# Feed-forward products with the high and low input halves side by side, 512 columns at a time

## The reference

```python
def swiglu(x, w_in, w_out):
    gate, up = jnp.split(x @ w_in, 2, axis=-1)
    return (jax.nn.silu(gate) * up) @ w_out

h = swiglu(rmsnorm(x, norm_ffn1_pre[l]), w_ffn1_in[l], w_ffn1_out[l])
x = x + FFN_RESIDUAL_SCALE * rmsnorm(h, norm_ffn1_post[l])
```

## Time and profile before

| | |
|---|---|
| median of 3 runs | 1515.03 us (1514.87 to 1515.17) |
| the profiled execution's own time | 1514.94 us |
| its span, first to last instruction | 1513.3 us |
| granted TensorE clock, mean of the span | 1.000 |
| the nine pairs of the first stage | about 60 to 241 us of the span |
| the nine pairs of the second stage | about 635 to 816 us |

### The profile page before, as it was taken

The page is one execution under the profiler, slowest core; times in us unless marked ns, Lnnn a source line. Parts: engine busy times, 40 slices in busy tenths (PEclk is TensorE's granted clock), DMA queues, the critical chain, the costliest instruction groups (busy, mean ns, idle before and its releaser), DMA issues.

```text
span 1513.3 us, 23600 instructions
## 1 busy us (share of the span) xinstructions
PE 1497.9 (99%) x9156; PEld 1343.9 (89%) x9156; DVE 1071.1 (71%) x1279; ACT 744.2 (49%) x1102; POOL 54.2 (4%) x101
## 2 busy tenths in 40 slices
PE   8999999999999999999999999999999999999998
PEld 7899998889988889899999888788888888889997
DVE  5888885326856847888886665788888865736873
ACT  6545443226566427544444234567676633344554
POOL 1000000001200002000000000100000000000001
PEclk9999999999999999999999999999999999999999
DMA  6233323232232222233335663222223132322331
GB/s 198 84 112 101 96 81 140 89 105 84 69 103 84 82 101 69 87 109 93 102 111 195 236 208 84 57 65 74 57 82 83 56 111 84 112 85 87 107 112 56
DMA packets 135044, 153.33 MB, mean 101 GB/s; under 512 B 3728, under 2 KB 123660, under 8 KB 134972
## 3 DMA queue, kind: packets, MB, share of 16 engines
q1 hardware_dynamic: 131712, 137.38, 28.9%
q0 software_dynamic: 3024, 14.88, 2.9%
q10 hardware_dynamic: 236, 0.06, 0.0%
HBM read 150.08 MB, written 2.23 MB: 101 GB/s over the span
## 4 chain that ended last, share of the span: by engine, by line
PE 96%; DVE 2%; ACT 1%; issue 0%; DMA 0%; DVEq 0%; ACTq 0%
PE ps L2532 20%; PE ps L2697 20%; PE ps L2534 19%; PE ps L2533 19%; PE ps L2702 10%; PE ps L2897 1%; PE ps L3003 1%; PE ps L3013 1%; PE ps L2983 1%; PE ps L2982 1%; PE ps L3012 1%; PE ps L2615 0%; PE ps L2964 0%; PE ps L2675 0%; DVE wl L1544 0%
## 5 line engine op out<-in xcount | busy, mean ns | idle before, releaser
L2532 PE MATMUL ps<-ah,wh 128*128 128x512 f32 (+1 forms) x1136 | 431.7, 380 | 3.8 <-DVE wl L1945 1.4
L2534 PE MATMUL ps<-ah,wl 128*128 128x512 f32 (+1 forms) x1136 | 425.6, 375 | 0.0
L2533 PE MATMUL ps<-al,wh 128*128 128x512 f32 (+1 forms) x1136 | 425.2, 374 | 0.0
L1544 DVE TENSOR_TENSOR wl<-raw,wh 128x2048 fp32r<-128x2048 f32 x59 | 135.2, 2291 | 191.2 <-ACT wh L831 191.0
L2532 PEld LDWEIGHTS ps<-ah,wh 128*128 128x128 f32 x1136 | 213.9, 188 | 43.3 <-issue 2.3
L2534 PEld LDWEIGHTS ps<-ah,wl 128*128 128x128 f32 x1136 | 213.8, 188 | 38.9
L2533 PEld LDWEIGHTS ps<-al,wh 128*128 128x128 f32 x1136 | 214.1, 188 | 35.5
L831 ACT ACTIVATE wh<-raw 128x2048 fp32r<-128x2048 f32 x60 | 114.7, 1911 | 236.7 <-PE ps L2534 233.0
L2697 PE MATMUL ps<-al,wh 128*128 128x256 f32 x704 | 172.7, 283 | 0.0
L2697 PE MATMUL ps<-ah,wh 128*128 128x256 f32 x704 | 172.7, 283 | 0.0
L2697 PEld LDWEIGHTS ps<-al,wh 128*128 128x128 f32 x704 | 135.2, 192 | 0.1
(11 more groups left out here) (436 smaller groups left out, 2535.6 us busy)
## 6 DMA issues: line engine op xcount, KB each, us to landing
raw<-in_w_ffn_in SPq DMA_DIRECT2D x74, 512.0 KB, 3.6
raw<-in_w_in SPq DMA_DIRECT2D x52, 512.0 KB, 4.4
raw<-in_w_ffn_out SPq DMA_DIRECT2D x22, 1024.0 KB, 5.0
ada_raw<-in_w_ada POOLq DMA_DIRECT2D x8, 1536.0 KB, 7.2
raw<-in_w_mix_in SPq DMA_DIRECT2D x10, 1024.0 KB, 5.4
raw<-in_w_ffn_in SPq DMA_DIRECT2D x7, 1024.0 KB, 5.3
raw<-in_w_in SPq DMA_DIRECT2D x6, 1024.0 KB, 5.6
raw<-in_w_mix_out SPq DMA_DIRECT2D x4, 1024.0 KB, 5.0
```

The source lines that it names most:

```text
L1544: nc.vector.tensor_tensor(wl[n % 2][:], raw[n % 2][:], wh[n % 2][:].bitcast(fp32), ALU.subtract).then_inc(lo_done, 2 if n + 1 in AHEAD else 1)
L2532: nc.tensor.matmul(bank, w[0], m[0], start=start, stop=False, skip_group_check=shared)
L2533: nc.tensor.matmul(bank, w[0], m[1], start=False, stop=False, skip_group_check=shared)
L2534: return nc.tensor.matmul(bank, w[1], m[0], start=False, stop=stop, skip_group_check=shared)
```

## The change

For the two feed-forward stages (not for the pairs of the second block), the high and the low input stand side by side in one buffer. In B11, T2, T3 and T4 one matmul of 512 columns takes both, high to the left and low to the right half of a whole bank; the low weight's matmuls go to the left half. So the result stands in two banks (0 and 1, or 6 and 7, one for each 128 result columns) and in two sides, which have to be added:

- for up1 and gate1 ScalarE copies both sides out, and GpSimd adds the second to the first (`sides`);
- for gate2 VectorE joins in two steps, the second waiting for the first (`sided_join`);
- for the last product ScalarE copies the low side to a new tile `whole2` (`last_side`), VectorE adds the high side, waits for that, and multiplies.

B22, T1 and B21 stay as they are. The out slot's first pass takes the banks in another order. The core of the diff:

```diff
+SIDE = 6
-        ah = sb("ah", [P, KD, T], f32r)
-        al = sb("al", [P, KD, T], f32r)
+        both = sb("both", [P, 2, KD, T], f32r)
+        ah, al = both[:, 0], both[:, 1]
...
+            both_sums = sb("both_sums", [P, 2, 3, KD // 2, T // 2], f32r, where=phase)
+            sh, sl = both_sums[:, 0], both_sums[:, 1]
+            whole2 = sb("whole2", [P, 2, T // 2], where=phase)
+        up1_side, gate1_side = (tile[:].rearrange("p (c t) -> p c t", c=2) for tile in (acc, h7))
...
+        def high_side(par):
+            return ps[:, SIDE * par:SIDE * par + 2, 0:T // 2]
+        def low_side(par):
+            return ps[:, SIDE * par:SIDE * par + 2, T // 2:T]
+        def both_of(f, name):
+            if name == "T3":
+                return both_sums[:, :, 1, :, :]
+            low, high = slice(0, KD // 2), slice(KD // 2, KD)
+            return both[:, :, high if name == "T4" else low, COLS[name != "B11"]]
@@ GpSimd @@
+            def sides(f):
+                first = SEVEN_AT[f]
+                def added(i, n, step, tile, side):
+                    pool.wait_ge(copied, i * 6 + (3 * n + step))
+                    nc.gpsimd.tensor_tensor(tile[:], tile[:], side, ALU.add).then_inc(side_added, 1)
+                def pair(i, par):
+                    n = first + par
+                    added(i, n, 1, up1, up1_side)
+                    added(i, n, 3, gate1, gate1_side)
...
+            sides(0)
             pool.wait_ge(rlo_done, 2)
...
             add_residual(3)
+            sides(1)
@@ ScalarE @@
+                def last_side(i, par):
+                    act.wait_ge(hid_ready, i * 2 + (f * NFO + PLAIN[f] + par))
+                    nc.scalar.activation(whole2[:], low_side(par % 2), ACT.Copy).then_inc(side_copied, 1)
+                    def sided_product(target, side):
+                        nc.scalar.activation(target[:], high_side(par % 2), ACT.Copy)
+                        nc.scalar.activation(side, low_side(par % 2), ACT.Copy).then_inc(copied, 1)
                         used(0)
+                        last_side(i, par - 1)
-                    product(up1, BANK1[par % 2])
+                    sided_product(up1, up1_side)
-                    product(gate1, BANK1[par % 2])
+                    sided_product(gate1, gate1_side)
...
                 act.wait_ge(p_used, PRODS * (last + 1))
+                last_side((SEVEN[f] - 1) // 2, (SEVEN[f] - 1) % 2)
                 hi(base_out + 1)
@@ VectorE, hidden(), second half @@
-                        nc.vector.tensor_tensor(at, ps[:, BANK1[par % 2], :].rearrange("p (c t) -> p c t", c=2), at, ALU.mult).then_inc(hid_ready, 1)
+                        dve.wait_ge(side_copied, i * 2 + (n + 1))
+                        nc.vector.tensor_tensor(whole2[:], high_side(par % 2), whole2[:], ALU.add).then_inc(last_joined, 1)
+                        dve.wait_ge(last_joined, i * 2 + (n + 1))
+                        nc.vector.tensor_tensor(at, whole2[:], at, ALU.mult).then_inc(hid_ready, 1)
@@ VectorE, pair() @@
+                    def sided_join(tile):
+                        nc.vector.tensor_tensor(tile[:], high_side(par % 2), tile[:], ALU.add).then_inc(high_joined, 1)
+                        dve.wait_ge(high_joined, i * 2 + (n + 1))
+                        nc.vector.tensor_tensor(tile[:], low_side(par % 2), tile[:], ALU.add).then_inc(joined, 1)
                     dve.wait_ge(copied, i * 6 + (3 * n + 3))
+                    dve.wait_ge(side_added, i * 4 + (2 * n + 2))
                     join(gate1, BANK5)
-                    join(gate2, BANK1[par % 2])
+                    sided_join(gate2)
@@ TensorE @@
+            def sided(f, i, n, k, par):
+                moving = both_of(f, PRODUCTS[k])
+                for nb in range(2):
+                    for kk in range(KD // 2):
+                        nc.tensor.matmul(ps[:, SIDE * par + nb, :].rearrange("p (s t) -> p s t", s=2), ring_of(wh, f, k)[:, kk, nb * P:(nb + 1) * P],
+                                         moving[:, :, kk, :], start=k == 0 and kk == 0, stop=False, skip_group_check=True)
+                pe.wait_ge(p_lo, i * 2 * PRODS + (PRODS * n + k + 1))
+                for nb in range(2):
+                    for kk in range(KD // 2):
+                        last = nc.tensor.matmul(ps[:, SIDE * par + nb, 0:T // 2], ring_of(wl, f, k)[:, kk, nb * P:(nb + 1) * P], moving[:, 0, kk, :],
+                                                start=False, stop=kk == KD // 2 - 1, skip_group_check=True)
+                last.then_inc(p_used, 1)
...
+                    if f < 2 and name in ("B11", "T2", "T3", "T4"):
+                        sided(f, i, n, k, par)
+                        continue
...
-                unit(0, first=True, blocks=[6, 7, 2, 3, BANK1[SEVEN[f] % 2], BANK5, BANK2, BANK1[1 - SEVEN[f] % 2]], before=free)
+                earlier, later = SIDE * (SEVEN[f] % 2), SIDE * (1 - SEVEN[f] % 2)
+                unit(0, first=True, blocks=[2, 3, earlier, earlier + 1, BANK5, BANK2, later, later + 1], before=free)
```

More of the change, by code:

```diff
@@ L212, in program @@
                 xl = sb("xl", [P, SLOT], f32r, where=inner)
-            sh = sb("sh", [P, 3, KD // 2, T // 2], f32r, where=phase)
-            sl = sb("sl", [P, 3, KD // 2, T // 2], f32r, where=phase)
+            both_sums = sb("both_sums", [P, 2, 3, KD // 2, T // 2], f32r, where=phase)
+            sh, sl = both_sums[:, 0], both_sums[:, 1]
             t4 = sb("t4", [P, KD // 2, CB], where=phase)
             ada = sb("ada", [P, 3 * D], where=phase)
+            whole2 = sb("whole2", [P, 2, T // 2], where=phase)
         with ExitStack() as phase:
@@ L334, in program @@
         copied, joined, gate_ready, gate_silu, half_done = sem("copied"), sem("joined"), sem("gate_ready"), sem("gate_silu"), sem("half_done")
+        side_copied, side_added, high_joined, last_joined = sem("side_copied"), sem("side_added"), sem("high_joined"), sem("last_joined")
         rhi_done, rlo_done = sem("rhi_done"), sem("rlo_done")
@@ L760, in ada_load @@
                 pool.dma_start(ada_raw[:, b, :, :], WAD[:, 4 * b:4 * b + 4, bass.ds(i * ADA, ADA)]).then_inc(ada_in[b], 16)
+            def sides(f):
[7 more added lines that the diff above has]
+                    added(i, n, 3, gate1, gate1_side)
+                pair(0, 0)
+                pair(0, 1)
+                with pool.Fori(1, SEVEN[f] // 2) as i:
+                    pair(i, 0)
+                    pair(i, 1)
+                if SEVEN[f] % 2:
+                    pair(SEVEN[f] // 2, 0)
+            sides(0)
             pool.wait_ge(rlo_done, 2)
@@ L1017, in product @@
                     def product(target, bank):
-                        nc.scalar.activation(target[:], ps[:, bank, :].rearrange("p (c t) -> p c t", c=2), ACT.Copy).then_inc(copied, 1)
+                        nc.scalar.activation(target[:], by_pair(ps[:, bank, :]), ACT.Copy).then_inc(copied, 1)
+                    def sided_product(target, side):
+                        nc.scalar.activation(target[:], high_side(par % 2), ACT.Copy)
+                        nc.scalar.activation(side, low_side(par % 2), ACT.Copy).then_inc(copied, 1)
                     def gate(h):
@@ L1824, in join @@
                     def join(tile, bank):
-                        nc.vector.tensor_tensor(tile[:], ps[:, bank, :].rearrange("p (c t) -> p c t", c=2), tile[:], ALU.add).then_inc(joined, 1)
+                        nc.vector.tensor_tensor(tile[:], by_pair(ps[:, bank, :]), tile[:], ALU.add).then_inc(joined, 1)
                     def scaled(tile, h):
@@ L2802, in free @@
                         pe.wait_ge(joined, 3 * (SEVEN_AT[f] + SEVEN[f]))
-                    elif c == BANK1[1 - SEVEN[f] % 2]:
+                    elif c == earlier:
+                        pe.wait_ge(hid_ready, (f + 1) * NFO - 1)
+                    elif c == later:
                         pe.wait_ge(hid_ready, (f + 1) * NFO)
-                unit(0, first=True, blocks=[6, 7, 2, 3, BANK1[SEVEN[f] % 2], BANK5, BANK2, BANK1[1 - SEVEN[f] % 2]], before=free)
+                earlier, later = SIDE * (SEVEN[f] % 2), SIDE * (1 - SEVEN[f] % 2)
+                unit(0, first=True, blocks=[2, 3, earlier, earlier + 1, BANK5, BANK2, later, later + 1], before=free)
                 with pe.Fori(0, 4) as i:
```

## The result

The change made the kernel slower: 1541.43 us (median of 4 runs, 1541.02 to 1541.85) against 1515.07 us, a ratio of 1.0174 with a 95% interval of 1.0159 to 1.0190. The forecast was 1537.1 us with a range of 1519 to 1549.

The account below looks back on a forecast made before the run. TensorE bounds the kernel, but VectorE's loop of 21.4 us a pair would take over. Per stage +0.35 first pair, +9.9 eight pairs, +0.8 end make 11.1, twice 22.2: 1514.94 + 22.2 = 1537.1 us, range 1519 to 1549.

Parts of the forecast that it names:

- VectorE's loop: VectorE's work and waits in each feed-forward pair: 19.87 us alone, already level with TensorE's 19.73.
- TensorE's part: Feed-forward pairs: four changed products of 2.773 us and three of 2.88 make 19.73 us a pair instead of 20.16.
- GpSimd's holds: GpSimd's two adds stop VectorE's two-SBUF-input instructions: 0.5 us at the gate product, 1.0 in the low parts, 1.5 a pair.
- The loop: VectorE's time a pair including the 1.5 us lost to GpSimd's adds: 21.4 us, against TensorE's 19.73.
- Where TensorE is stopped: T4 waits for gate2 to be joined: the next 17 of the 18 T4s wait, some 1.7 us each.
- First pair and end: Each stage: first T4 at 77.65 instead of 77.3, +0.35 us; after the last join 3.65 us of VectorE work, +0.8.
- The rest: ScalarE's three more copies (at most 1.8 us a pair), SP's loads, GpSimd's queue and buffer placement: hidden, cost nothing.
- The banks' order: The out slot's new order of banks costs nothing: its last two wait 4.1 us in, about 2.1 needed.
- GpSimd does not hold VectorE: Rival, chance 0.11: GpSimd's adds cost VectorE nothing, loop under about 19.9 us, time about 1508 us.
- One add escapes: Rival, chance 0.10: one GpSimd add does not hold VectorE, loop 20.4 to 20.9 us, time 1520 to 1529 us.
- both hold in full: Rival, chance 0.13: both GpSimd adds hold VectorE fully, loops of 21.9 to 22.0 us, time 1543 to 1547 us.
- TensorE's clock fell: Rival, chance 0.02: TensorE's clock falls when it waits in every pair, time above 1550 us.

Follow-up runs that it names:

- the narrow run: Changed kernel with each matmul of 512 columns again two of 256 into the two sides, nothing else different: 1541.23 us, ratio 1.0172 to the kernel before.

## Why the prediction was right, point by point

The mechanism came out as forecast: VectorE's loop, lengthened by GpSimd's two adds, sets the pace, and TensorE waits at T4. Two sizes in it were short, both to the same side.

- **TensorE's part.** The step "four of them and three of 2.88 make 19.73 us" was slightly off: a sided product takes 2.80 us in the traces, not 2.773 (232.58 to 235.38 in the changed kernel), so a pair takes 19.84. That it doesn't matter in the changed kernel was right, and the narrow run shows it.
- **VectorE's loop** was put at 19.87 us without holds and is 20.14. Two starts were later than counted: difference T3, which overwrites what low part 1 reads, starts 1.26 us behind it instead of 1.135 (124.74 to 126.00), and the new product starts 0.83 behind its add (183.95 to 184.78), not 0.72. Together they are 0.24 of the 0.27 us. The first could have been read from the kernel before (119.88 to 121.14 there). The second is more than the wait for the add: in the last pair of the stage the same two instructions start 0.72 apart (237.69 to 238.41). The trace has a register instruction for the product's line in 12 of the 18 pairs:

```profile
L1865 DVEq FUSED_REGOPS  x12: 57/64/65, 107.8 to 804.7; - x12
```

  That it makes the 0.11 us was not tried. The two waits for ScalarE came out as predicted, 1.23 and 0.51 us counted from start to start.
- **GpSimd's holds** were put at 1.5 us (0.5 and 1.0) and are 1.62 to 1.63 (0.53 and 1.09). Both places are as worked out: GpSimd begins at 129.08, 1.94 us after L1857 (1.95 predicted), the add with the PSUM input goes through, the product behind it pays; the second hits the run of low parts. In the second stage the product takes 1.16 us instead of 1.22, and the loop is 21.70 us. Holds of all 1.29 us, as the rule of the Trainium skill had it, would have given 2.0 us; in these rows VectorE goes on 0.14 us before GpSimd's recorded end and so pays less.
- **The loop** is therefore 21.77 and not 21.4 us, and this is the term that was mis-sized: eight pairs of the first stage take 251.51 - 77.68 = 173.83 us, 2.6 more than eight times 21.4, and eight of the second 839.51 - 666.52 = 172.99 us, 1.8 more. The profiled execution took 1541.79 us, 4.7 over the sum of 1537.1. Of these the loop makes 4.4; TensorE's slow clock at the end of the first stage adds 0.8 (below), and the first T4 of the second stage takes 0.6 back.
- **Where TensorE is stopped:** T4, 17 times, up to 1.75 us, as said; T2 never waited.
- **First pair and end.** The first T4 of stage one started at 77.68, predicted 77.65. In the second stage the first T4 did not wait: it started 666.52 - 649.52 = 17.00 us after B11, where six plain products take 17.28 and the sum had 17.63, so 0.6 us were counted too many. The end took 3.60 us from T4 to the out slot in the second stage (3.65 predicted):

```profile
649.52 1.98 PE L2748 MATMUL ps<-both,wh 128*128 128x512 f32 x8
...
666.52 2.00 PE L2748 MATMUL ps<-both,wh 128*128 128x512 f32 x8
...
839.51 2.14 PE L2748 MATMUL ps<-both,wh 128*128 128x512 f32 x8 [1.75 <-DVE gate L1892]
843.11 0.50 PE L2596 MATMUL ps<-both,wh 128*128 128x512 f32 x1 [0.52 <-DVE wl L1871]
```

- **The rest** at nothing: ScalarE's three copies and GpSimd's queue show in no wait of TensorE's in the pairs. The banks' order showed none either.
- **The rivals.** That GpSimd does not hold VectorE is refuted by four runs: none, one or both adds, and the adds on VectorE itself. That rival's price was right in kind, a time under the kernel before's, but too low: without holds the time was 1512.5 us, where the rival said 1508, since VectorE's loop of 20.14 us is above TensorE's 19.84 even then. "One add escapes" did not come about, nor did "both hold in full", though the loop of 21.77 us is nearer to its 21.9 than to the 21.4 of the forecast. TensorE's clock fell once in this trace and cost about 0.8 us (below); that rival's price was a time above 1550 us.

## What to carry to other kernels

An engine that is 71% busy over the span can be within 3 us of its limit in the stage that matters: add up its loop there, with each wait that it keeps and each instruction that must wait for the one before. An add handed to GpSimd isn't free for VectorE: while GpSimd reads SBUF, VectorE's instructions with two SBUF inputs stand still, here for 0.5 and 1.1 us a pair, where the two adds on VectorE itself take 0.6 each. When wider matmuls make TensorE faster, first make room on the engine behind it (fill its waits by changing the order), and then take the gain: the four wide products cost 26 us as they were first put in, and brought 4.4 with the adds on VectorE and the two orders of work changed.

## What the runs showed that was not expected

- A GpSimd instruction that only writes held nobody: a memset of 0.52 us inside a VectorE subtraction of two SBUF tiles lengthened neither. A GpSimd add of only four elements did wait for VectorE's instruction to end (0.68 us instead of 0.20).
- TensorE's clock: in the changed kernel's last pair of the first stage, after a wait of 1.75 us, eight wide matmuls took 3.0 us (251.51 to 254.53) where the other pairs take 1.9. The windows (length, TensorE busy, granted clock as a share of 2.4 GHz, DMA share, GB/s) of the stretch before it, of this stretch and of two us within it show that for a part of it TensorE ran at its lower level of 1.2 GHz:

```profile
238.00:250.00 12.00, 11.76 (x84) 1.00 0.52 176
250.00:258.00 8.00, 6.49 (x25) 0.79 0.19 49
253.00:255.00 2.00, 2.00 (x8) 0.50 0.00 0
```

  The 16 other waits of this kernel before T4, one of them 1.75 us long too, left no such mark, and the narrow version, with waits of up to 1.4 us, had 1.00 in the first two windows; its profiled execution was 0.7 us shorter (1541.12 against 1541.79). The out slot came 4.47 us after T4 here and 3.60 in the second stage, so the fall cost at most 0.9 us. The four times of the changed kernel lie in two groups, 1541.0 to 1541.1 and 1541.8 to 1541.9, which would fit a fall in some executions and not in others; only one of them has a trace. What sets it off was not tried.
